# The first projection and the first attention of a one-core transformer kernel, put in another order

## What is computed

```python
h = rmsnorm(x, ln1_g[l])                      # x * rsqrt(mean(x*x) + eps) * g
proj = h @ w_in[l]                            # 1024 x 5120
qa, ka, va, qb, kb, vb, ga, gb = jnp.split(proj, offsets, axis=-1)
qa = apply_partial_rope(rmsnorm(qa.reshape(B, S, DIL_HEADS, HEAD_DIM), q_norm_a[l]), cos, sin)
...
oa = dilated_attention(qa, ka, va)            # 12 heads in 3 groups, combined to 4
ob, _ = banded_attention(qb[:, None], kb[:, None], vb[:, None], SWA_WINDOW - 1, sinks[l])
mix = jax.nn.sigmoid(ga) * (oa @ w_branch_a[l]) + jax.nn.sigmoid(gb) * (ob @ w_branch_b[l])
x = x + mix @ w_out[l]
h2 = rmsnorm(x, ln2_g[l])
x = x + jnp.square(jax.nn.relu(h2 @ w_up[l])) @ w_down[l]
```

## Time and profile before

| | us |
|---|---|
| median of three runs | 1406.83 (1404.22 to 1409.38) |
| the profiled execution | 1404.03 |
| its span, first to last instruction | 1402.4 |
| busy in it: TensorE | 1346.8 (96%) |
| VectorE | 829.3 (59%) |
| ScalarE | 619.4 (44%) |
| GpSimd | 73.8 (5%) |

### The profile page before, as it was taken

How to read it: one execution, slowest core, us unless ns; L and a number is a source line. 1 busy time by engine, 2 the same in 40 slices (tenths; PEclk the granted TensorE clock), 3 DMA queues, 4 the chain that set the end, 5 groups by cost and what they waited for, 6 DMA issues and landing times.

```text
span 1402.4 us, 15837 instructions
## 1 busy us (share of the span) xinstructions
PE 1346.8 (96%) x6430; PEld 1091.8 (78%) x6430; DVE 829.3 (59%) x1128; ACT 619.4 (44%) x841; POOL 73.8 (5%) x132
## 2 busy tenths in 40 slices
PE   6998899999999999999999999999999999999997
PEld 5876677888887888886678888888888866788886
DVE  5674465645455544588785554664455877755445
ACT  4644534535235334435634433354434366353341
POOL 3321000000000000000110000000000002000000
PEclk9999999999999999999999999999999999999999
DMA  7651144655556555544266565565565441666550
GB/s 263 195 173 60 61 162 154 210 182 180 199 169 208 193 189 182 187 171 121 61 204 216 184 191 195 180 210 180 188 195 188 150 121 61 232 198 195 185 180 30
DMA packets 149336, 238.55 MB, mean 170 GB/s; under 512 B 5472, under 2 KB 97648, under 8 KB 149264
## 3 DMA queue, kind: packets, MB, share of 16 engines
q1 hardware_dynamic: 148880, 237.00, 51.8%
q0 software_dynamic: 384, 0.54, 0.2%
HBM read 236.47 MB, written 1.05 MB: 169 GB/s over the span
## 4 chain that ended last, share of the span: by engine, by line
PE 71%; issue 17%; DVE 4%; ACT 3%; DVEq 2%; POOL 2%; POOLq 1%; DMA 1%; SPq 0%; ACTq 0%
PE ps L1302 22%; PE ps L1304 21%; PE ps L1303 21%; PE ps L1555 2%; DVE stats L1068 1%; ACT whi L406 1%; PE ps L1348 1%; PE ps L1341 1%; PE ps L1342 1%; POOLq L425 1%; POOL lrs L431 1%; PE ps L1407 1%; POOL drs L426 1%; DVE wlo L411 1%; DVEq L1067 1%
## 5 line engine op out<-in xcount | busy, mean ns | idle before, releaser
L411 DVE TENSOR_TENSOR wlo<-raw,whi 128x2048 fp32r<-128x2048 f32 x217 | 491.3, 2289 | 154.0 <-ACT whi L406 154.0
L1302 PE MATMUL ps<-whi,xt_hi 128*128 128x512 f32 (+1 forms) x1064 | 424.4, 399 | 3.2 <-DVE wlo L411 2.6
L1304 PE MATMUL ps<-whi,xt_lo 128*128 128x512 f32 (+1 forms) x1064 | 412.8, 388 | 0.0
L406 ACT ACTIVATE whi<-raw 128x2048 fp32r<-128x2048 f32 x217 | 407.9, 1915 | 10.6 <-DMA raw<-in_w_up_dram 5.8
L1303 PE MATMUL ps<-wlo,xt_hi 128*128 128x512 f32 (+1 forms) x1064 | 411.8, 387 | 0.0
L1302 PEld LDWEIGHTS ps<-whi,xt_hi 128*128 128x128 f32 x1064 | 200.3, 188 | 52.1 <-issue 12.2
L1304 PEld LDWEIGHTS ps<-whi,xt_lo 128*128 128x128 f32 x1064 | 200.3, 188 | 41.9
L1303 PEld LDWEIGHTS ps<-wlo,xt_hi 128*128 128x128 f32 x1064 | 200.6, 189 | 36.2
L1302 PE MATMUL ps<-whi,ht_hi 128*128 128x512 f32 x480 | 187.6, 391 | 0.0
L1303 PE MATMUL ps<-wlo,ht_hi 128*128 128x512 f32 x480 | 186.8, 389 | 0.0
L1304 PE MATMUL ps<-whi,ht_lo 128*128 128x512 f32 x480 | 186.8, 389 | 0.0
(11 more groups left out here) (178 smaller groups left out, 1042.6 us busy)
## 6 DMA issues: line engine op xcount, KB each, us to landing
raw<-in_ffn_w_in_dram SPq DMA_DIRECT2D x176, 512.0 KB
raw<-in_ffn_w_out_dram SPq DMA_DIRECT2D x44, 1024.0 KB
raw<-in_w_in_dram SPq DMA_DIRECT2D x38, 1024.0 KB
raw<-in_w_up_dram SPq DMA_DIRECT2D x16, 1024.0 KB
raw<-in_w_down_dram SPq DMA_DIRECT2D x16, 1024.0 KB
raw<-in_w_out_dram SPq DMA_DIRECT2D x8, 1024.0 KB
ln_g<-in_ln_g_dram SPq DMA_DIRECT2D x8, 512.0 KB, 6.8
raw<-in_w_out_dram SPq DMA_DIRECT2D x8, 512.0 KB
```

The costliest lines, as they stand in the source:

```text
L406: act.activation(whi[j][:, :], raw[j][:, :], ACT.Copy).then_inc(hi_done, 1)
L411: dve.tensor_tensor(wlo[j][:, :], raw[j][:, :], whi[j][:, :].bitcast(F32), ALU.subtract).then_inc(lo_done, 1)
L1302: pe.matmul(o, hi[:, k, tok], block_of(whi, u, b, width), start=start, stop=False)
L1304: return pe.matmul(o, lo[:, k, tok], block_of(whi, u, b, width), start=False, stop=stop)
```

## The change

**Head.** x is no longer scaled ahead of the transposes. The gain comes as 8 rows of 128 numbers (`g_rows`, 4 KB), PE turns it into a column for each block (`g_cols`), and the weights of w_in (units 0 to 19) are multiplied by it while they are split: each split is four operations of 128x512 with a column as factor. The reciprocal root is applied where ACT reads the strips out of their banks (`lrs`, and half of it, `hrs`, for the gates). SP loads token tile 0, the gain, units 0 and 1 in halves, and then token tile 1. PE multiplies token tile 0 in pairs of blocks, `lo hi` ahead of `hi lo`. It runs 12 transposes of the identity before the gain, and 6 before the first matmul, whose results nobody reads. POOL issues the constants' DMAs after the second unit's high half is done (`hi_done` 2), and makes the reciprocal roots after them. The gain of the second norm is loaded without a wait.

**Attention.** Scores always stand in banks 2 and 3, turned probabilities in 4 and 5, outputs in bank 6, other transposes in bank 7. Step i has scores(i), the turning of i-2, the outputs of i-3. Scores wait for maxima(i-1), the turning for the copy of the unit before. The fill is in pieces of three matmuls for one token tile (`gate_piece`), in two groups a step, and three pieces stand among the first transposes. The windowed units run all of token tile 0 first. The last head norm, the turning of the windowed queries, of branch a's and half of branch b's heads, and branch a's matmuls are moved into the steps; the units' splits are moved in the same way, and unit 23 is split there too.

```diff
 S1_SOLID = 7
-STEP_BLOCKS = (1, 1, 1, 1, 1, 1, 1, 1, 1, 1, 2, 2, 2, 2, 2, 2, 2, 0)
-STEP_SPLITS = {2: 16, 5: 17, 8: 18, 10: 19, 12: 20, 14: 21, 16: 22}
+
+
+QK1_FILL, GATE_FILL, BRANCH_FILL = 1, (3,) * 13 + (2,) * 3, {16: 3, 17: 3, 18: 2}
+STEP_HI = {0: 16, 2: 17, 5: 18, 7: 19, 9: 20, 11: 21, 13: 22, 16: 23}
+STEP_LO = {2: 16, 4: 17, 6: 18, 8: 19, 10: 20, 13: 21, 15: 22, 17: 23}
+SQUARES_3, SUMS_3, NORM_3, TURN_QB, TURN_OA, TURN_OB0 = 0, 1, 3, 5, 12, 16
...
         @block.sync
         def _(sp):
-            for t in range(TT):
-                sp.dma_start(xres[:, t, :], x_r[:, t, :]).then_inc(x_loaded[t], 16)
-            sp.dma_start(ln_g[:, :], ln1_g[0, :].partition_broadcast(P)).then_inc(g_loaded, 16)
-            for s in range(S1):
+            sp.dma_start(xres[:, 0, :], x_r[:, 0, :]).then_inc(x_loaded[0], 16)
+            sp.dma_start(g_rows[:, :], ln1_g[0, :].rearrange("(k p) -> k p", p=P)).then_inc(g_rows_loaded, 16)
+            for u in range(2):
+                sp.dma_start(rows_of(u)[:, 0:2, :], w_in_r[:, 4 * u:4 * u + 2, 0:BW]).then_inc(half_loaded[u], 16)
+                sp.dma_start(rows_of(u)[:, 2:4, :], w_in_r[:, 4 * u + 2:4 * u + 4, 0:BW]).then_inc(loaded[SLOT_OF[u]], 32)
+            sp.dma_start(xres[:, 1, :], x_r[:, 1, :]).then_inc(x_loaded[1], 16)
...
+        def scaled_hi(act, u, blocks):
+
+            j = SLOT_OF[u]
+            for b in blocks:
+                cols, k = slice(b * BW, (b + 1) * BW), 4 * (u % 2) + b
+                m = act.activation(whi[j][:, cols], raw[j][:, cols], ACT.Copy, scale=g_cols[:, k:k + 1])
+            return m
...
+        def half_split_hi(act, u, h):
+
+            act.wait_ge(half_loaded[u] if h == 0 else loaded[SLOT_OF[u]], 16 if h == 0 else 32)
+            scaled_hi(act, u, (2 * h, 2 * h + 1)).then_inc(half_hi if h == 0 else hi_done, 1)
+
...
             pool.memset(ident[:, :], 0.0)
             pool.drain()
             pool.affine_select(out=ident[:, :], in_=ident[:, :], compare_op=ALU.not_equal, fill=1.0,
                                base=0, pattern=[[-1, P]], channel_multiplier=1).then_inc(ident_ready, 1)
-            rms_pool(pool, 0)
+            pool.memset(half[:, :], -0.5)
+            pool.memset(one_lam[:, :, :], 1.0)
+            pool.wait_ge(hi_done, 2)
...
             pool.iota(dist[:, :], [[1, P]], base=P, channel_multiplier=-1).then_inc(consts_set, 1)
             pool.drain()
+            rms_pool(pool, 0)
+            pool.drain()
+            pool.tensor_scalar(hrs[:, :], lrs[:, :], 0.5, None, ALU.mult).then_inc(half_rstd, 1)
             pool.wait_ge(mask_mod, 1)
...
         @block.scalar
         def _(act):
-            for t in range(TT):
-                act.wait_ge(x_loaded[t], 16)
-                rms_act(act, 0, (t,))
-            split_hi(act, 0)
-            xt_act(act, 0, toks=(0,))
-            split_hi(act, 1)
+            xt_act(act, 0, toks=(0,), halves=(0,))
+            act.wait_ge(g_ready, 1)
+            half_split_hi(act, 0, 0)
+            xt_act(act, 0, toks=(0,), halves=(1,))
+            half_split_hi(act, 0, 1)
+            for h in range(2):
+                half_split_hi(act, 1, h)
+            rms_act(act, 0, (0,))
             xt_act(act, 0, toks=(1,))
             for s in range(S1_SOLID):
                 if s > 0:
                     read_proj1(act, s - 1)
                 for j in range(2):
                     split_hi(act, 2 * s + 2 + j)
...
             reads = gate_reads()
-            for i in range(UNITS + 2):
-                if i in reads:
-                    read_gate(act, reads[i])
-                if i == 3:
+            for i in range(UNITS + 3):
+                for strip_tile in reads.get(i, ()):
+                    read_gate_tile(act, *strip_tile)
...
-                if 1 <= i <= UNITS:
-                    read_pt(act, i - 1)
-                if i in STEP_SPLITS:
-                    split_hi(act, STEP_SPLITS[i])
-            xt_act(act, 1, 6)
-            split_hi(act, U_WOUT1)
+                if 0 <= i - 2 < UNITS:
+                    read_pt(act, i - 2)
+                if TURN_QB <= i < TURN_QB + 3:
+                    read_qk(act, (6 + i - TURN_QB,))
+                if i == TURN_OA:
+                    branch_a_act(act)
+                if i == TURN_OB0:
+                    branch_b_act(act, 0)
...
-            rms_dve(dve, 0)
-            split_lo(dve, 0)
-            xt_dve(dve, 0, toks=(0,))
-            split_lo(dve, 1)
+            dve.wait_ge(g_turned, 1)
+            dve.tensor_copy(g_cols[:, :], ps[:, 0, 0:KD]).then_inc(g_ready, 1)
+            dve.drain()
+            xt_dve(dve, 0, toks=(0,), halves=(0,))
+            half_split_lo(dve, 0, 0)
+            xt_dve(dve, 0, toks=(0,), halves=(1,))
+            half_split_lo(dve, 0, 1)
+            for h in range(2):
+                half_split_lo(dve, 1, h)
             xt_dve(dve, 0, toks=(1,))
             for s in range(S1_SOLID):
...
+        def pairs_of_first_tile(pe, q, what):
+
+            o, tok, u = ps[:, 0, :], slice(0, P), q // 2
+            if what == "hi hi":
+                pe.wait_ge(hi_done if q % 2 else half_hi, u + 1)
+                pe.wait_ge(xt_hi_done, u + 1)
...
+                w = wlo if what == "hi lo" else whi
+                pe.matmul(o, x[:, k, tok], block_of(w, u, k % 4), start=what == "hi hi" and k == 0,
+                          stop=what == "hi lo" and k == KD - 1)
+
+        def first_projection(pe):
+
+            pairs_of_first_tile(pe, 0, "hi hi")
+            pairs_of_first_tile(pe, 0, "lo hi")
+            pairs_of_first_tile(pe, 1, "hi hi")
+            pairs_of_first_tile(pe, 1, "lo hi")
+            pairs_of_first_tile(pe, 0, "hi lo")
+            pairs_of_first_tile(pe, 2, "hi hi")
+            pairs_of_first_tile(pe, 2, "lo hi")
+            pairs_of_first_tile(pe, 1, "hi lo")
+            pairs_of_first_tile(pe, 3, "hi hi")
+            pairs_of_first_tile(pe, 3, "lo hi")
+            pairs_of_first_tile(pe, 2, "hi lo")
+            for b in range(2):
+                xt_half_pe(pe, 0, 1, b, xres)
+            pairs_of_first_tile(pe, 3, "hi lo")
+            first_tile(pe, 0, 0, 1, 1)
+
...
         def turn_probs(pe, u):
             pe.wait_ge(e_ready, u + 1)
-            s = set_of(u)
+            if u >= 1:
+                pe.wait_ge(pt_out, u)
             for j in range(width_of(u) // P):
-                m = pe.transpose(s[:, j * P:(j + 1) * P], ebuf1[u % 3][:, j * P:(j + 1) * P], ident[:, :])
+                m = pe.transpose(turned1[:, j * P:(j + 1) * P], ebuf1[u % 3][:, j * P:(j + 1) * P], ident[:, :])
             m.then_inc(pt_ready, 1)
...
                     m = pe.matmul(dst, pt[:, j * P:(j + 1) * P], v, start=i == 0, stop=i == len(terms) - 1)
             m.then_inc(o_ready, 1)
+
+        def gate_piece(pe, p):
+
+            s, t, k = S1_SOLID + p // (2 * KD), p // KD % 2, p % KD
+            if k == 0:
+                pe.wait_ge(proj_out, 2 * s - 1 + t)
+            if t == 0 and k % 4 == 0:
+                pe.wait_ge(lo_done, 2 * s + k // 4 + 1)
+            m = tile_mm(pe, xt_hi, xt_lo, k, 2 * s + k // 4, k % 4, t, t, k == 0, k == KD - 1)
+            if t == 1 and k % 4 == 3:
+                m.then_inc(used, 1)
+            if t == 0 and k == KD - 1:
+                m.then_inc(gate_tile, 1)
+
...
             pe.wait_ge(ident_ready, 1)
+            for _ in range(12):
+                pe.transpose(ps[:, 3, 0:P], ident[:, :], ident[:, :])
+            pe.wait_ge(g_rows_loaded, 16)
+            pe.transpose(ps[:, 0, 0:KD], g_rows[:, :], ident[0:KD, 0:KD]).then_inc(g_turned, 1)
             for b in range(2):
-                xt_half_pe(pe, 0, 0, b, normed)
-            first_strip(pe, 0, normed, 0, 2)
+                xt_half_pe(pe, 0, 0, b, xres)
+            for _ in range(6):
+                pe.transpose(ps[:, 3, 0:P], ident[:, :], ident[:, :])
+            first_projection(pe)
             strip(pe, 2, pair(1))
             for s in range(2, S1_GATES + 1):
...
-                    pe.wait_ge(qk_out, 6)
-                if i == UNITS // 2:
-                    pe.wait_ge(roped, 4)
-                    pe.wait_ge(o_out, i - 2)
-                    qk_pe(pe, range(6, QK1_BANKS), 6, 2)
-                    pe.wait_ge(qk_out, QK1_BANKS)
+            for i in range(UNITS + 3):
+                n_fill = GATE_FILL[i] if i < UNITS else BRANCH_FILL[i]
+                piece = gate_piece if i < UNITS else branch_a_piece
+                if i == UNITS:
+                    p = 0
                 if i < UNITS:
                     scores(pe, i)
-                if 1 <= i <= UNITS:
-                    turn_probs(pe, i - 1)
-                if i >= 2:
-                    outputs(pe, i - 2)
-                for b in blocks[i]:
-                    s = S1_SOLID + b // KD
-                    if b % KD == 0:
-                        pe.wait_ge(proj_out, 2 * s)
-                    strip_block(pe, 2 * s, b % KD, pair(0))
```

(11 more changed lines are left out.)

265 lines of the change are left out of this document (181 added, 84 removed).

## The result

| | before | after |
|---|---|---|
| median of the runs side by side (lowest to highest) | 1408.11 (1404.22 to 1409.72) | 1381.51 (1381.09 to 1381.69) |
| ratio, 95% interval | | 0.9818 (0.9801 to 0.9835) |
| the profiled execution | 1404.03 | 1381.67 |
| its span | 1402.4 | 1379.8 |

The account below looks back on a forecast made before the run. TensorE's stream was taken as the bound, with time to win only where it waits or runs at low clock. Head 8.5 plus attention 11 (18 - 3.9 - 2.9) made 19.5 off 1406.83: 1387.3 us, range 1382 to 1395.

Parts of the forecast that it names:

- What was hidden there and now may not be: Behind the head: splits 0.45 longer on DVE fit the solid strips; constants landing late could cost 2.2 us, taken as 0.
- A DVE wait on the constants and a TensorE wait on wlo at 32: Sign of being wrong: DVE waits for the constants' DMAs ahead of the angles, TensorE for low weights at 32.
- The stall: Attention: six TensorE waits for ACT's copy of the turned probabilities, 11.0 of 15.7 us of waits, were to go.
- what is late next: Attention: waits left once the stall goes, from gate read, short steps, turned queries and mix; 2.9 us, between 1 and 6.
- Each group of fill costs 0.09 going in ... and, I take, as much going out: 0.19 ... +3.9: Attention: price of splitting the fill into about 20 more groups, 0.19 us each, 3.9 us lost.
- the cover: Attention: steps of 5.1 us on average exceed DVE's 4.4 and ACT's 4.6, and results have a step more.
- The same gain from that: The sum: 19.5 us taken off the median 1406.83, which is 2.8 above the profiled execution, giving 1387.3.
- (a): Head: idle transposes don't bring the clock up, the first strip ends 2.1 us later, 1389.4; chance 0.20.
- (b): Attention: waits return through DVE's and ACT's strict queues, half the gain, 5.5 us, goes, 1393; chance 0.14.
- (c): Behind the head: constants land at 26.2 and hold strip 2 for 2.2 us, 1389.5; chance 0.08.
- (d): Attention: short fill groups leave TensorE at half clock, slower than before, 1421 if all at low clock; chance 0.04.
- (e): Attention: waits on the single score or output bank serialise steps, 1.2 us each over 16, 1407; chance 0.04.

Follow-up runs that it names:

- e4: Changed kernel with each step's fill in one group behind the outputs; 1380.02 us, ratio 0.9814.
- e5: Changed kernel with probabilities turned one step behind the scores, not two, and outputs two, not three; 1380.94 us, ratio 0.9819.
- e12: e5 with the bank roles of the kernel before: scores in two alternating pairs, probabilities turned in place; 1383.82 us, ratio 0.9845.
- e2: Changed kernel with the head of the kernel before, so the attention part alone; 1386.78 us, ratio 0.9865.
- e1: Kernel before with only the head of the change, its attention left as it was; 1406.43 us, ratio 1.0001.
- e11: Changed kernel's head with the attention of before, plus 88 idle transposes in the attention's waits; 1402.23 us, ratio 0.9971.
- e10: Kernel before with 88 idle transposes ahead of the six scores that wait for the probabilities' copy; 1402.57 us, ratio 0.9974.
- e8: Changed kernel with 24 idle transposes in the wait before the second norm's transposes; 1380.34 us, ratio 0.9814.

## Why the prediction was right, and where it was off

**The head, 8.5 forecast, 8.55 in the trace.** First matmul at about 8 (7.98), second strip at 20.7 to 21 (20.87). Within it one size was off at no cost: ACT's halves took 1.26 to 1.32 and not 1.1, so that its last was done at 12.08 and not 11.5, but DVE, which comes behind, was done at 13.95 where 13.9 was forecast. The solid strips, which I had at no cost, lost 0.5. "What was hidden there and now may not be" counted the longer splits and the landing of the constants, and not that POOL's reciprocal roots now stand behind the issues of these constants: ACT waited 3.8 for them at 25.31, and strip 2 came 0.2 late at 32.13. A DVE wait on the constants and a TensorE wait on wlo at 32 had been named as a sign of being wrong: the first did not come, the second did, small and by another cause.

**The attention, 11 forecast, 14.9 in the trace.** The stall went as forecast, from 11.0 to 0.5, and what is late next was forecast well: the last gate read 0.8 (0.8), the turned queries 0.5 (0.6), one short step 0.5 (twice 0.5), the mix nothing (0.5), and 0.5 on a copy that the list did not have; 2.3 in all against 2.9. The failed step is "Each group of fill costs 0.09 going in ... and, I take, as much going out: 0.19 ... +3.9". Going out to the turning costs nothing, and e4 measures 0.055 for a group, 1.1 for twenty. That is 2.8 of the 3.9 us between 14.9 and 11; 0.6 are the waits, 0.3 is rounding (the terms add up to 11.3), and 0.2 is not traced.
The reason given for the cover was wrong too, though it moved no number: "each result now has a step more until it is asked for". e5 takes the step away and loses nothing, and e12 shows own banks to be worth 2.8 of the 15.4 between before and e5.

**The sum from the median.** "The same gain from that" took the 2.8 us between profiled execution and median of before as an offset that stays. It goes with the low clock, which differs from run to run in the kernel before, and it went with the waits: after, the profiled execution and the median are 0.2 apart. How much of it lies in the attention is not shown run by run. Of the 5.8 us between forecast and measured median, this is 2.8; another 2.8 stands in the traces already (1384.5 forecast, 1381.67 taken), and 0.2 is that last distance. Together they put the time below the range.

**The parts are not additive.** The sum treated head and attention as independent. In the trace of after each stage gave about its share, but beside e2 the head is worth 5.3 to 6.6 us in the medians and not 8, and e1 gains nothing alone, by the clock and by the longer splits. "What was hidden there and now may not be" named the longer splits and looked for their cover in the solid strips alone; in the attention of before there was none.

**The rivals.** (a) idle transposes don't bring the clock up: out. After eight transposes of x, one of the gain and 12 of the identity, and during the last six, the clock rose, at 7.68, ahead of every 128x512 matmul. The Trainium skill's rule in "TensorE: Matmul & The Clock Gate", PE-mode transpose, that a transpose doesn't count as a busy engine for the clock, does not hold for these fp32 transposes: without the 18 of the identity (e3) the clock rose at 13.02. It is not certain to be in time: in e11, with the same 18, it rose at 10.6, behind the first 128x512 matmuls (8.19). e10 points the same way in the attention; e8 does so more weakly, since e10 kept its clock at that place without them. (b) the waits return under other names: 2.3 us in all, out. (c) late constants: DVE's cast at 23.39 waited for nothing, out; the 0.2 us at 32.13 come from POOL's order, as said above. (d) half clock from the short groups: the granted clock of the attention was 1.00. (e) serialised by the single banks: one wait of 0.5 on the maxima.

## To carry to other kernels

An engine that waits a few us again and again may also lose its clock, and differently from run to run, for a reason that these traces do not show. Compare the mean granted clock over all runs before taking a profiled execution as typical (it misses the time before the clock first rises: before's first strip has 1.00 in that column, with half clock until 20.45), and add the clock's loss to what a wait costs. A part that gains nothing alone (a shorter head with longer splits) can be worth most of its price once the stage behind it no longer waits for the engines that it loads; test parts alone and together. When an engine's work is moved behind something else, ask who waits for its results: POOL's roots held nobody before the change, and held ACT after it. Idle transposes in a wait with a known end are a cheap way to hold the clock, where a bank is free.
